# One decoder step (RG-LRU, sparse attention, mixture of experts): prompt attention over selected and recent keys set among the gate projections, the compressed keys' part added later

## The reference, cut to what matters

```python
def nsa_attend(q, pos, cmp_k, cmp_v, gather_slc, nsb, win_k, win_v, win_pos, gates):
    ...
    p_c = masked_softmax(s, cmp_end <= pos[:, None, None, None])
    o_cmp = jnp.einsum('nqhgc,nchd->nqhgd', p_c.astype(cmp_v.dtype), cmp_v)
    ...
    g = jax.nn.sigmoid(gates)
    return g[..., 0:1] * o_cmp + g[..., 1:2] * o_slc + g[..., 2:3] * o_win

def merge_branches(y_lru, o_nsa, ga, gb, w_proj_a, w_proj_b, w_out):
    return (jax.nn.sigmoid(ga) * (y_lru @ w_proj_a) + jax.nn.sigmoid(gb) * (o_nsa @ w_proj_b)) @ w_out
```

## Time and profile before

| | us |
|---|---|
| median of 3 runs | 2096.61 |
| the runs | 2094.52 to 2097.3 |
| the profiled execution, its own time | 2103.45 |
| its span, first to last instruction | 2101.7 |

### The profile page before, as it was taken

How to read it: one execution, slowest core, us unless ns; L and a number is a source line. 1 busy time by engine, 2 the same in 40 slices (tenths; PEclk the granted TensorE clock), 3 DMA queues, 4 the chain that set the end, 5 groups by cost and what they waited for, 6 DMA issues and landing times.

```text
span 2101.7 us, 26584 instructions
## 1 busy us (share of the span) xinstructions
PE 2005.5 (95%) x8807; PEld 1532.9 (73%) x8807; DVE 1380.9 (66%) x1617; ACT 1061.6 (51%) x993; POOL 208.9 (10%) x165
## 2 busy tenths in 40 slices
PE   7999999888999999969999999999999999999996
PEld 4478654666588884447888888888888888888885
DVE  3433620466310002369999999999999999999994
ACT  2113310345000001247877777777868777877773
POOL 0010210000000000230101101010101010110100
PEclk9999999679799999859999999999999999999998
DMA  8141131112241214239999999999999999999992
GB/s 343 50 164 41 48 94 50 50 49 86 80 174 40 100 41 162 105 116 360 363 390 379 381 376 374 393 368 385 366 396 358 400 365 392 374 377 380 376 378 68
DMA packets 82667, 514.59 MB, mean 245 GB/s; under 512 B 10297, under 2 KB 43121, under 8 KB 55073
## 3 DMA queue, kind: packets, MB, share of 16 engines
q1 hardware_dynamic: 67728, 460.48, 55.5%
q0 software_dynamic: 14736, 52.78, 9.7%
q10 hardware_dynamic: 144, 0.55, 0.1%
HBM read 490.93 MB, written 28.24 MB: 247 GB/s over the span
## 4 chain that ended last, share of the span: by engine, by line
PE 76%; DVE 7%; issue 7%; ACT 7%; DMA 2%; POOL 1%; ACTq 0%; DVEq 0%; POOLq 0%; SPq 0%
PE bank L858 24%; PE bank L442 14%; PE bank L872 13%; PE bank L535 5%; PE bank L476 4%; PE bank L759 3%; ACT qT_rounded L1133 3%; PE bank L840 2%; PE bank L834 1%; PE bank L649 1%; ACT wide_rounded L1133 1%; PE bank L629 1%; PE bank L720 1%; DVE slab L1692 1%; DVE slab L1695 1%
## 5 line engine op out<-in xcount | busy, mean ns | idle before, releaser
L1672 DVE TENSOR_TENSOR ring_rounded<-ring,wide_rounded 128x2048 fp32r<-128x2048 f32 x192 | 433.1, 2287 | 36.7 <-ACT wide_rounded L1133 36.7
L858 PE MATMUL bank<-ring_rounded,slab_rounded 128*128 128x512 f32 x1024 | 401.1, 392 | 0.0
L1133 ACT ACTIVATE wide_rounded<-ring 128x2048 fp32r<-128x2048 f32 x192 | 357.9, 1904 | 3.8 <-PE bank L858 3.8
L858 PE MATMUL bank<-xn_rounded,slab_rounded 128*128 128x512 f32 x1024 | 327.7, 391 | 2.2 <-DVE ring_rounded L1672 2.2
L1672 DVE TENSOR_TENSOR ring_rounded<-ring,xn_rounded 128x2048 fp32r<-128x2048 f32 x128 | 292.8, 2288 | 20.4 <-ACT xn_rounded L1133 20.4
L872 PE MATMUL bank<-wide_rounded,slab_rounded 128*128 128x512 f32 x768 | 259.0, 398 | 0.0
L858 PE MATMUL bank<-wide_rounded,slab_rounded 128*128 128x512 f32 x768 | 247.2, 389 | 0.0
L1133 ACT ACTIVATE xn_rounded<-ring 128x2048 fp32r<-128x2048 f32 x128 | 243.5, 1903 | 0.0
L442 PE MATMUL bank<-xn,ring 128*128 128x260 f32 x1024 | 228.6, 383 | 0.6 <-ACT wide L941 0.6
L858 PEld LDWEIGHTS bank<-xn_rounded,slab_rounded 128*128 128x128 f32 x1024 | 193.5, 189 | 42.5 <-ACT xn_rounded L1133 2.7
L858 PEld LDWEIGHTS bank<-ring_rounded,slab_rounded 128*128 128x128 f32 x1024 | 192.7, 188 | 41.5
(11 more groups left out here) (352 smaller groups left out, 2435.1 us busy)
## 6 DMA issues: line engine op xcount, KB each, us to landing
ring<-in_w_exp SPq DMA_DIRECT2D x192, 2048.0 KB, 10.5
ring<-in_w_ch SPq DMA_DIRECT2D x8, 2048.0 KB, 24.2
slab<-in_w_tok SPq DMA_DIRECT2D x4, 1304.0 KB, 15.2
ring<-in_k_cmp SPq DMA_DIRECT2D x64, 64.0 KB, 1.8
ring<-in_w SPq DMA_DIRECT2D x2, 2048.0 KB, 8.6
ring<-in_k_slc SPq DMA_DIRECT2D x64, 64.0 KB, 1.8
ring<-in_v_slc SPq DMA_DIRECT2D x64, 64.0 KB, 1.8
ring<-in_w_pa SPq DMA_DIRECT2D x2, 2048.0 KB, 8.4
```

Source lines behind the costliest of these rows:

```text
L858: r = mm(bank[:, c, :], a[:, 4 * h + k, :], w[:, k, :], start=False, stop=h == 1 and k == 3 and x == 2)
L1133: fn(WH[(2 * c + h) % 6], ring[:, half_of(c, h)], ACT.Copy).then_inc(S["wh_ready"], 1)
L1672: v.tensor_tensor(ring_r[:, half_of(c, h)], ring[:, half_of(c, h)], WHf[(2 * c + h) % 6], ALU.subtract)\
```

## The change

The changed kernel's line numbers differ: the gate pieces are on its line 536, `scores` on 595, `turn` on 616 to 624, `values` on 644, the page loop on 363 to 367.

- The list of items now has, for each query tile, the eight `full` items and an `out`; the four `cmp` items, each with a `sum`, come at the list's end. `OA` is started by the first `full` item, `cmp` writes to a buffer `OC`, and `sum` adds it to `oT` on DVE.
- The 256 gate products are cut into 64 pieces of four. Sixteen pieces run ahead of the attention, and 48 in it: one per `full` item of the first and last query tile, two per `full` item of the two between. The attention stage stands ahead of the hidden layer of `compress`; the four `cmp` items come after that layer.
- `PT` (the transposed weights) has one buffer where it had two, and the `values` of a `full` item land in the PSUM bank that `turn` writes, so that `turn` of the next item waits for DVE's `outputs` of the last.
- The tanh of the gates are taken in the attention stage and kept in `SGA` (ring slot 5 and a piece of `qf`) and `SGB` (in `slab`). The loop at the end holds the projections alone, and `pa` of tile m waits for `m_ready` of tile m-2.
- The ring plan has five slots and explicit slot numbers, and SP's order of loads is another.

```diff
-    return [("ar0", 1), ("ag0", 1), ("ar1", 1), ("ag1", 1),
...
+    return [("ar0", 0, 1), ("ag0", 1, 1), ("ar1", 2, 1), ("ag1", 3, 1), ("ga0", 4, 1), ("ga1", 0, 1), ("gb0", 1, 1), ("gb1", 2, 1),
+            ("xsk", 3, 2), ("w1k", 0, 1), ("xsv", 1, 2), ("w1v", 3, 1), ("kwin", 4, 1), ("kslc", 0, 2), ("vslc", 2, 2),
+            ("vwin", 4, 1), ("pa0", 0, 1), ("pa1", 1, 1), ("pb", 2, 1), ("wo0", 3, 1), ("wo1", 4, 1)]
...
+        eslot = [0, 1, 2, 5, 3, 4]
...
+        SGB = [mT[:, m, :] for m in range(KD)]
+        SGA = [ring[:, 5 * SLOT + m * NT:5 * SLOT + (m + 1) * NT] for m in range(KD - 1)] + [qf[:, 2040:2040 + NT]]
...
+        FIRST_PIECES = 16
+        want = [(1 if x[1] in (0, QT_N - 1) else 2) if x[0] == "full" else 0 for x in items[:NFULL]]
+        upto = [min(64, FIRST_PIECES + sum(want[:i])) for i in range(NFULL + 1)]
...
+            load("ga0", d["w_ch"][4])
+            load("ga1", d["w_ch"][5])
+            load("gb0", d["w_ch"][6])
+            load("gb1", d["w_ch"][7])
             load_pages("xsk", d["k_cmp"], S["xsk_in"])
             load("w1k", d["w1"][0])
             load_pages("xsv", d["v_cmp"], S["xsv_in"], NPAGES // 2)
             load("w1v", d["w1"][1])
-            load_pages("kslc", d["k_slc"], S["kslc_in"])
-            load_pages("vslc", d["v_slc"], S["vslc_in"])
             slots_free("kwin")
             sp.dma_start(chunk("kwin").rearrange("p (n k) -> p n k", n=NSA), d["k_win"])\
                 .then_inc(ring_in[slot_of["kwin"]], 16)
+            load_pages("kslc", d["k_slc"], S["kslc_in"])
+            load_pages("vslc", d["v_slc"], S["vslc_in"])
             slots_free("vwin")
...
+            def gate_piece(x):
+                j, part = divmod(x, 2)
+                n, h = divmod(j, 2)
+                m = n % KD
+                name = ("ga", "gb")[n // KD] + str(m // 4)
+                if part == 0:
+                    if m % 4 == 0 and h == 0:
+                        pe.wait_ge(ring_in[slot_of[name]], count_of[name])
+                    if j >= 2:
+                        pe.wait_ge(S["gate_out"], j - 1)
+                for k in range(4 * part, 4 * part + 4):
+                    r = mm(bank[:, 6 + h, 0:HN], w8(name)[:, k, (m % 4) * P:(m % 4 + 1) * P], xn[:, k, h * HN:(h + 1) * HN],
+                           start=k == 0, stop=k == KD - 1)
+                if part:
+                    r.then_inc(S["gate_done"], 1)
...
+            for i in range(NFULL):
+                pieces = range(upto[i], upto[i + 1])
+                if i >= 1:
+                    values(i - 1)
+                if i + 1 < NFULL:
+                    scores(i + 1)
+                for x in pieces[0:1]:
+                    gate_piece(x)
+                turn(i)
+                for x in pieces[1:2]:
+                    gate_piece(x)
...
             for m in range(KD):
...
+                name = f"pa{m // 4}"
+                if m % 4 == 0:
+                    pe.wait_ge(ring_in[slot_of[name]], count_of[name])
+                if m >= 2:
+                    pe.wait_ge(S["m_ready"], m - 1)
+                merged(name, 2 + m % 2, m, Y, KD).then_inc(S["pa_done"], 1)
+                if m == 0:
+                    pe.wait_ge(S["smp_dve"], 7)
+                    pe.transpose(bank[0:HD, 0, 0:NROW], oS[R, :], ident[R, R]).then_inc(S["smp_pe"], 1)
+                    pe.wait_ge(ring_in[slot_of["pb"]], count_of["pb"])
+                else:
+                    if m == 1:
+                        pe.wait_ge(S["smp_dve"], 8)
+                    merged("pb", m % 2, m - 1, oT, NG).then_inc(S["pb_done"], 1)
```

More of the change, by code:

```diff
@@ L308, in build @@
         for qt in range(QT_N):
-            items.append(("cmp", qt, 0, 0))
             full = [("full", qt, b, g) for b in (1, 2) for g in range(NG)]
-            items += full[0:1] + ([("out", qt - 1, 0, 0)] if qt else []) + full[1:]
-        items.append(("out", QT_N - 1, 0, 0))
+            items += full + [("out", qt, 0, 0)]
+        NFULL = len(items)
+        for qt in range(QT_N):
+            items += [("cmp", qt, 0, 0)] + ([("sum", qt - 1, 0, 0)] if qt else [])
+        items.append(("sum", QT_N - 1, 0, 0))
+        NALL = len(items)
         n_full = [sum(x[0] == "full" for x in items[:i + 1]) for i in range(len(items))]
@@ L346, in build @@
         before = {}
[L347 to L349 removed]
+        for name, first, n in ring_plan():
+            sl = range(first, first + n)
             before[name] = [owner[x] for x in sl if x in owner]
@@ L352, in build @@
                 owner[x] = name
-            jj += n
+        chunk_free = [frees[owner[x]] if x in owner else (S["m_ready"], KD) for x in eslot]
         def some_pages(eng, dst, pool, signal, first, n):
@@ L553, in _, with scores @@
             pe.wait_ge(S["ag_gelu"], KD)
+            def scores(i):
+                kind, qt, b, g = items[i]
+                if kind in ("out", "sum"):
+                    return
+                if i >= 2 and items[i - 2][0] == "full":
+                    pe.wait_ge(S["att_p"], n_full[i - 2])
+                elif i >= 2 and items[i - 2][0] == "cmp":
+                    pe.wait_ge(S["att_pc"], n_cmp[i - 2])
+                s0 = 2 * (i % 2)
+                q = slice(qt * P, (qt + 1) * P)
+                for kv in range(NKV):
+                    r0 = slice(HD * kv, HD * (kv + 1))
+                    if kind == "cmp":
+                        for gg in range(NG):
+                            r = mm(bank[:, s0 + kv, gg * 32:gg * 32 + 32], qT[r0, gg, q], ckTp[r0, :], start=True, stop=True)
+                    else:
+                        r = mm(bank[:, s0 + kv, 0:(qt + 1) * P], qT[r0, g, q], kT[r0, b, 0:(qt + 1) * P],
+                               start=True, stop=True)
+                r.then_inc(S["att_s"], 1)
@@ L1330, in prompt_rows @@
+            maxima(0)
+            for i in range(NFULL):
+                if i >= 1:
+                    outputs(i - 1)
+                if i + 1 < NFULL:
+                    maxima(i + 1)
+                weights(i)
             def prompt_rows(vv):
```

540 lines of the change are left out of this document (267 added, 273 removed).

## The result

| | before | after |
|---|---|---|
| median of 4 runs | 2096.95 us | 2208.36 us |
| the runs | 2094.52 to 2103.59 us | 2203.96 to 2208.79 us |
| the profiled execution, its own time | 2103.45 us | 2203.96 us |
| its span | 2101.7 us | 2202.2 us |

The ratio after to before is 1.0521 (95% interval 1.0494 to 1.0549): the changed kernel is 5.2% slower. The forecast was 2199.5 us, 9 us under the median, with the range 2174 to 2230 us. The kernel before runs at one of two levels, 2094 to 2099 us (mean granted clock 0.960 to 0.962) or 2102 to 2105 us (0.956 to 0.959), and its profiled execution is one of the longer ones.

A forecast was written before the change was run, and what follows sets the result against it. The prediction took TensorE's work and waits to bound the kernel at 245 to 793 us, and late page loads afterwards. Its terms put the output projection at 896 against 793.3: +103 on 2103.45, 2206, less 6.8: 2199.5 us; range 2174 to 2230.

The forecast's parts named there:

- (1): Gates and attention as the new first stage: 213 us, between 192 and 240, so `hidden_samples(0)` starts at 458.4.
- (2): Hidden layer of `compress`: unchanged at 122.9 us, so `cs_done` 8 comes at 581.3.
- (3): Sample rows: page loads start only at `cs_done` 8 and, not TensorE, set this stretch; `vwin` is in at 772.
- (4): Sample rows, from `vwin` to the end of `vslc`'s values: 25.5 us, ending at 797.7.
- (5): Last loop: `pb` load, 77.9 us of products and waits of `pa` for `m_ready`; 98.4 us, output projection at 896.
- the step on the bare copy: Attention: with one piece per item the wait for ScalarE's copy stays exposed, 13 us in all; two pieces cover it.
- The second rival: Gates and attention: interleaving fails and the clock stays at 0.78; 54 us more, 2253 us; chance 0.06.
- The third: Gates and attention simply add: 232 us with the ends, 19 more than forecast, 2219 us; chance 0.08.
- The first rival: Page loads are paced by memory, not issue; both loads and `vwin` take some 50 us; 2089 us; chance 0.04.
- The last term: Sample rows: `vwin` behind both page loads, 0.6 + 10.8 us of issues, last piece landing some 6 us on.
- 81 us: TensorE's work while the page loads run: prompt part and second layer 21, four `cmp` items 25, sample scores 35.
- part 3: The cached keys and values (`kslc`, `vslc`, then `vwin`) moved behind the hidden layer; `vwin` in at 772, wanted at 662.

The follow-up runs named there:

- experiment nine: Changed kernel with one gate piece per item in the first two query tiles and two in the last two; 2199.0 us, ratio 1.0469.
- experiment three: Changed kernel with all 64 gate pieces ahead of the attention and none in it; 2272.26 us, ratio 1.0825.
- one: Changed kernel with `kslc` and `vslc` each as one contiguous 4 MB load instead of a page loop, page table left out; 2119.59 us, ratio 1.0096.
- two: Changed kernel with half of the `kslc` and `vslc` pages issued by SyncE and the other half by GpSimd; 2121.33 us, ratio 1.0093.
- experiment four: Changed kernel with `pa` waiting only for its PSUM bank to be read and `pb` for `m_ready` three tiles earlier; 2191.67 us, ratio 1.0433.
- experiment five: Changed kernel with page loads split over SyncE and GpSimd and other ring slots, so `kslc` loads during the values' hidden layer; 2127.05 us, ratio 1.0135.

## Why the prediction was right, and where it was not

The predicted time line against the changed kernel's trace:

| step | predicted | trace |
|---|---|---|
| (1) `hidden_samples(0)` starts | 458.4 | 461.9 |
| (2) second sample part ends (`cs_done` 8) | 581.3 | 581.1 |
| (3) `kslc` issued | 668.5 | 667.6 |
| (3) `vslc` issued | 755.2 | 756.3 |
| (3) window's values start | 772 | 766.9 |
| (4) end of `vslc`'s values | 797.7 | 792 |
| (5) output projection starts | 896 | 890.6 |

**(1) Gates and attention** came within 3.5 us. By tile an item was forecast at 3.4, 5.5, 6.5 and 6.7 us; the trace has 3.72, 5.61, 6.49 and 6.99. The assumption on which it stood, full clock once gate records stream, holds (0.99), and experiment nine confirms the step on the bare copy by moving a piece to it. The second rival (the clock stays at 0.78) is out by the same row. The third (attention and gates simply add, 232 us) is out by the trace, but it was asked of the old attention's 111 us: by experiment three the attention without pieces takes 292 - 113 = 179 us in the new order, and half clock is a large part of that.

**(2) The hidden layer** came right through two errors that cancel. It began 3.5 us late, and its two sample parts with the prompt part between them took 119.2 us instead of 122.9 in the profiled execution; between the sample parts lie 8.0 us, where the earlier trace rows has 311.50 - 300.33 = 11.2. In the changed kernel profiled again the second prompt part took 6.59 us instead of 3.79, and the two sample parts with it 124.7 us. So this is luck of the single execution, and it can be part of why the profiled one lies 4 us under the others.

**(3) The loads decide** was the forecast's main step, and it is what the runs show most plainly. The two waits were forecast at 30 to 40 and 60 to 80 us and measured 26.9 and 63.1; the first lies under its range, since TensorE had more work ahead of it (below). Taking the loops' pace away (one, two) takes 87 to 89 us away. The first rival (memory paces the pages) is out: 83.56 and 85.45 us for 64 pages in a stage where little else moves, and half of it with two issuers. The issue itself can be read in the chain of the changed kernel, one turn of the `kslc` loop, at the line of the register loads (L364) and the DMAs (L367):

```profile
592.14 0.27 SPq L364
...
592.81 0.26 SPq L364
...
594.83 0.34 SPq L367
...
595.48 0.34 SPq L367
```

Register loads follow each other at 0.65 us and DMA issues at 0.65 us, four of each to a turn: 5.2 us, or 1.3 us a page. That is how issue comes to be the limit. The Trainium skill ("DMA: Bandwidth & Descriptors", Latency and other measured facts) puts such a load at about 600 ns, and the trace agrees. The fit that the prediction takes from the Trainium skill ("DMA: Bandwidth & Descriptors", Anatomy of one DMA) is given there for DMAs issued from GpSimd, and these are SyncE's; experiment one's 4 MB landed in 12.2 and 14.2 us, not far from its 10. The last term was mis-sized: SyncE issued the window's values in 5.9 us, not 10.8, so they were in 5 us sooner than forecast, about what the bound named there allowed ("4 us less if vwin lands faster").

**The term that was wrong** is what TensorE has to do in that stretch, "81 us". With its waits for other engines it is 97: from 581.1 to 678.5 in experiment one. The four `cmp` items, put at 25 us ("my estimate from 7 to 9 us for one alone, two in flight"), take 37.5 (601.4 to 638.9). From there to the window's values it takes 39.5, put at 35, with the wait of 7.1 us for DVE in it. The timeline of experiment one shows why:

```profile
617.04 2.79 PE L597 MATMUL bank<-wide,qT 64*128 64x32 f32 x16
619.76 2.07 PE L642 MATMUL bank<-xn 128*128 128x256 f32 x4
621.63 1.06 PE L620 MATMUL bank<-ident,slab 128*128 128x128 f32 x4
625.87 0.66 PE L624 MATMUL bank<-ident,xn 128*128 128x128 f32 x2 [3.18 <-DVE oT L1458]
626.46 2.79 PE L597 MATMUL bank<-wide,qT 64*128 64x32 f32 x16
```

An item takes 9.4 us, and the next one's transposes wait 3.2 us for DVE, whose operations of two items stand one behind the other (rows of 0.43 and 0.70 us). TensorE does run the next item's scores ahead, but only the first two items overlap. This was hidden by the loads and so cost the forecast nothing. But the first rival, which rests on it, would have been 678.5 + 25.5 + 98.4 = 802.4 and some 2106, not 2089. Experiment one started its output projection there (801.70) and took 2114.95 in its profiled execution.

And it bears on the reading of the change: the sentence "the work saved is real: without part 3 the same line would end early" is wrong. Gates and all attention items cost nearly the same before and after: 113.4 + 143.7 = 257 us before, 216.5 + 37.5 = 254 after. These 3 us, and 5 us by which the hidden layer came out shorter in this execution, are mostly taken back by 6 us more in the sample rows, which is the wait for DVE. What the gate pieces fill, by the rows of experiment three, is the copy that the new order lays bare and the half clock; the late `cmp` items cost their own.

**(5) The last loop** came out as worked: 98.6 us against 98.4, with the six gaps at 1.59 us each; experiment four removes them and nothing else. The gaps and the loads come to 99.4 us of a loss of 97.3; the rest comes to 2 us less in these two executions.

The forecast's remaining 9 us below the median come from the step from profile to median: the profiled execution of before lay 6.8 us above its runs' median and 6.8 were taken off, while after's profiled execution lay 4.4 us below. So two profiled executions lay on opposite sides of their medians, and the 6.8 are the distance between the two levels of the kernel before. That the forecast fell inside its range doesn't rest on this. Besides, from the output projection's start to the end the changed kernel takes 1311.6 us and the kernel before 1308.4; these 3.2 us no experiment took apart. In the other kernels' traces it is 1308.1 to 1311.9 us, and the cause stays open.

## What to carry to other kernels

Before work is moved past a load, look whose slot the load waits for: a load keeps its length but loses its cover. Here 169 us of page issues came to stand where TensorE had 97 us to do. The plan of slots sets the start (experiment five moved it by 56 us), but no run changes the slots alone with the full page loops, so what that is worth by itself isn't shown. A page loop is paced by its issuer, so a second engine that issues half of it was worth nearly as much here as a contiguous load. Fill a stretch of short dependent products with independent ones; in these runs the clock rose with the filler (a third-tile item got shorter with 3.5 us of products more in it, and four `cmp` items took 28.3 us of products in 10). But count first what the filling order itself costs: here an item of the third tile cost 1.2 us more by itself. And before a difference of a few microseconds is put down to an edit, look at the same rows in a second execution of the same kernel.

## What the runs showed of the hardware

- The granted clock fell to 0.50 to 0.68 in attention windows in which TensorE was busy 74 to 83% (experiment three), and stood at 0.99 with gate products between (93% busy). The Trainium skill ("TensorE: Matmul & The Clock Gate", HAM oscillation) lays the half clock to idle gaps between bursts. The rows agree only in part: TensorE's pauses in these windows are 0.4 to 1.1 us each, and with the same pauses of 0.90 us the end of the third tile (463 to 472 us) was granted 0.96.
- The same instructions with the same pause ahead can run at either level. The second prompt part of the changed kernel took 3.79 us in one profiled execution and 6.59 in the other, both behind a pause of 0.74 us. From 521 to 531 us the one was granted 1.00 and the other 0.70. What decides it isn't settled here.
- Two engines that issue page DMAs at once hardly slow each other: 40.96 us for 32 pages on SyncE beside 41.7 for GpSimd's 32, where SyncE alone took 83.56 for 64.
